# A two-network float32 forward pass on one core: norm chains by half blocks, a merged slab of narrow weights, and moved splits and dummy matmuls

## The reference

```
def rms_norm(x, gain):
    xf = x.astype(jnp.float32)
    y = xf * lax.rsqrt(jnp.mean(xf * xf, axis=-1, keepdims=True) + EPS)
    return (y * gain).astype(x.dtype)

# first network
for layer in range(2):
    hn = rms_norm(h, attn_norm[layer])
    h = h + (hgrn2_mixer(hn, ...) if layer == 0 else dsa_mixer(hn, ...))
    h = h + conv_ffn(rms_norm(h, ffn_norm[layer]), ...)      # SwiGLU with a conv of width 3
x = rms_norm(h, final_norm)

# second network
for l in range(2):
    g = norm_g[l]
    f = swiglu(rms_norm(h, g[0]), ffn1_w_in[l], ffn1_w_out[l])
    h = h + 0.5 * rms_norm(f, g[1])
    hn = rms_norm(h, g[2])
    m = even_mixer(hn, ...) if l == 0 else odd_mixer(hn, ...)
    h = h + rms_norm(m, g[3])
    f = swiglu(rms_norm(h, g[4]), ffn2_w_in[l], ffn2_w_out[l])
    h = h + 0.5 * rms_norm(f, g[5])
```

## Time and profile before

| | |
|---|---|
| median of 3 runs | 1748.61 us (1748.54 to 1750.45) |
| profiled execution | 1750.39 us, span 1748.6 us |
[...]
| instructions | 28885 |
| read from HBM | 280.88 MB, 161 GB/s over the span |

### The profile page before, as it was taken

How to read it: one execution, slowest core, us unless ns; L and a number is a source line. 1 busy time by engine, 2 the same in 40 slices (tenths; PEclk the granted TensorE clock), 3 DMA queues, 4 the chain that set the end, 5 groups by cost and what they waited for, 6 DMA issues and landing times. The chain is left out here.

```text
span 1748.6 us, 28885 instructions
## 1 busy us (share of the span) xinstructions
PE 1681.4 (96%) x11818; PEld 1565.9 (90%) x11818; DVE 1060.8 (61%) x1495; ACT 846.7 (48%) x1138; POOL 114.0 (7%) x37
## 2 busy tenths in 40 slices
PE   7999999999999999999999879999999999899998
PEld 6998999989799998999989669998999989889997
DVE  1796776756667676544569854555545575765544
ACT  6323655543555455544465364345543465363443
POOL 5351000020700000000010000000000000000000
PEclk9999999989999999999999989999999999999999
DMA  8622477733245555455553225555455654425552
GB/s 270 203 73 97 146 209 210 206 120 115 79 157 169 194 184 173 158 192 187 200 169 131 96 80 190 176 190 193 157 185 182 209 162 142 145 96 181 192 184 80
DMA packets 220068, 283.49 MB, mean 162 GB/s; under 512 B 13004, under 2 KB 197315, under 8 KB 219987
## 3 DMA queue, kind: packets, MB, share of 16 engines
q1 hardware_dynamic: 218499, 278.18, 48.9%
q10 hardware_dynamic: 1488, 4.17, 0.7%
HBM read 280.88 MB, written 1.44 MB: 161 GB/s over the span
## 5 line engine op out<-in xcount | busy, mean ns | idle before, releaser
L1616 PE MATMUL ps<-x_hi,w_hi 128*128 128x256 f32 (+1 forms) x2368 | 673.9, 285 | 1.0 <-DVE x_lo L1018 1.0
L1617 PE MATMUL ps<-x_lo,w_hi 128*128 128x256 f32 (+1 forms) x2368 | 672.4, 284 | 0.0
L1618 PE MATMUL ps<-x_hi,w_lo 128*128 128x256 f32 (+1 forms) x2368 | 672.2, 284 | 0.0
L546 ACT ACTIVATE w_hi<-raw 128x2048 fp32r<-128x2048 f32 x262 | 498.8, 1911 | 206.3 <-PE ps L1618 197.1
L1127 DVE TENSOR_TENSOR w_lo<-raw,w_hi 128x2048 fp32r<-128x2048 f32 x162 | 371.3, 2292 | 260.3 <-ACT w_hi L546 260.3
L1616 PEld LDWEIGHTS ps<-x_hi,w_hi 128*128 128x128 f32 (+1 forms) x2368 | 456.2, 193 | 5.4 <-issue 3.2
L1617 PEld LDWEIGHTS ps<-x_lo,w_hi 128*128 128x128 f32 (+1 forms) x2368 | 456.2, 193 | 2.3
L1618 PEld LDWEIGHTS ps<-x_hi,w_lo 128*128 128x128 f32 (+1 forms) x2368 | 456.0, 193 | 0.2
L1616 PE MATMUL ps<-w_hi,x_hi 128*128 128x256 f32 (+3 forms) x688 | 225.2, 327 | 27.1 <-DVE x_lo L1018 19.7
L1617 PE MATMUL ps<-w_lo,x_hi 128*128 128x256 f32 (+3 forms) x688 | 219.3, 319 | 0.0
L1618 PE MATMUL ps<-w_hi,x_lo 128*128 128x256 f32 (+3 forms) x688 | 219.3, 319 | 0.0
(11 more groups left out here) (170 smaller groups left out, 1334.8 us busy)
## 6 DMA issues: line engine op xcount, KB each, us to landing
raw<-in_ffn_w_in SPq DMA_DIRECT2D x88, 1024.0 KB, 5.1
raw<-in_ffn_w_up SPq DMA_DIRECT2D x44, 1024.0 KB, 5.1
raw<-in_ffn_w_out SPq DMA_DIRECT2D x44, 1024.0 KB, 4.8
raw<-in_ffn_w_down SPq DMA_DIRECT2D x22, 1024.0 KB, 5.0
raw<-in_hgrn_w_in SPq DMA_DIRECT2D x16, 1024.0 KB, 5.9
raw<-in_gla_w_in SPq DMA_DIRECT2D x12, 1024.0 KB, 5.5
raw<-in_hyb_w_in SPq DMA_DIRECT2D x10, 1024.0 KB, 5.6
raw<-in_dsa_w_in SPq DMA_DIRECT2D x6, 1024.0 KB, 5.6
```

What stands on the lines that cost most here:

```text
L546: act.activation(w_hi[slot][:, :], raw[slot][:, :], ACT.Copy).then_inc(hi_done[slot], 1)
L1616: pe.matmul(out_ap, a_hi, b_hi, start=start, stop=False, skip_group_check=True)
L1617: pe.matmul(out_ap, a_hi, b_lo, start=False, stop=False, skip_group_check=True)
L1618: return pe.matmul(out_ap, a_lo, b_hi, start=False, stop=stop, skip_group_check=True)
```

## The change

- **Norm chains.** Additions to h, gains, updates and squares go by halves of 512 columns, with new semaphores h_half, y_half and rms_eps. PE finishes the first half of a block's last product before the second and says so. The sum of squares is held in two columns; DVE adds eps to the first (`add_eps`), and ACT's root takes the second with that as its bias.
- **Order.** `split_normed(1)` on ACT comes ahead of the table preload and, in `normed_ffn`, `high_one(c_)` ahead of the second block's square. In `after_ffn` DVE gains or adds block 1 before it splits block 0. The last low part of an FFN is made in two halves, the second behind the norms (`low_part`).
- **Sparse attention.** Slot 0 holds w_idx (8 columns) beside v, slot 1 k_idx twice; one call projects 136 columns, DVE takes both out of one bank.
- **FFN 3's first two slabs** get their high and low parts at the end of the hybrid mixer; there the low part of slot 3 comes after all of the convolution, and ACT makes x_hi between the Silu steps.
- **GLA.** Low parts after steps 10, 11 and 13 become slots 2 and 3 after step 13 and slot 0 after the whole of `linear_attention`.
- **Dummies.** Those ahead of the transposes after FFN 1 to 4 are gone. New: 8 ahead of the outputs of each linear attention, 7, 2 and 9 after the first transposes of the three turned output projections, 6 at the end of the sparse attention, and in the hybrid mixer 18, 4, 8, 16 and 8 instead of 8, 4 and 8. In FFN 2 and 4 and in the mixers after them the second block's transposes move to before the last two of eight contraction steps.

The core of the diff:

```diff
-NEXT_PIECES = (3, 1, 1, 1, 1)
+NEXT_PIECES = (2, 1, 1, 1, 1)
...
-            load(0, [(raw_cols(0, 0, 64), ki), (raw_cols(0, 64, 64), ki), (raw_cols(0, P, P), col_slab(dsa_in, DSA_V, P))])
-            load(1, [(raw_cols(1, 0, IDX_HEADS), col_slab(dsa_in, DSA_W, IDX_HEADS))])
+            load(0, [(raw_cols(0, 0, IDX_HEADS), col_slab(dsa_in, DSA_W, IDX_HEADS)),
+                     (raw_cols(0, IDX_HEADS, P), col_slab(dsa_in, DSA_V, P))])
+            load(1, [(raw_cols(1, 0, 64), ki), (raw_cols(1, 64, 64), ki)])
...
+            def square_half(tb, part, src, scale):
+                at = 2 * tb + part
+                act.activation(squares[:, part * 512:part * 512 + 512], src, ACT.Square, scale=scale, accum_out=ssq[:, at:at + 1])\
+                    .then_inc(rms_sq, 1)
+            def root_of_sum(tb):
+                act.wait_ge(rms_sq, want(rms_sq, 2))
+                act.wait_ge(rms_eps, want(rms_eps))
+                act.activation(std[:, tb:tb + 1], ssq[:, 2 * tb + 1:2 * tb + 2], ACT.Sqrt, bias=ssq_eps[:, tb:tb + 1])\
+                    .then_inc(rms_std, 1)
...
                 split_normed(0, *norm)
                 if after_out and last is not None:
                     square_product(1, last, half)
+                high_one(c_)
                 square_h(1, updates)
+                split_normed(1, *norm)
                 preload(ACT.Silu)
-                high_one(c_)
-                split_normed(1, *norm)
...
+            split_normed(1, "norm_g_2", 0)
             preload(ACT.Silu)
             high_one(FFN_SLOTS[2][2])
-            split_normed(1, "norm_g_2", 0)
...
+                        if c >= 1:
+                            conv_high(c - 1)
+                    conv_high(3)
+                    high_one(FFN_SLOTS[3][0])
+                    high_one(FFN_SLOTS[3][1])
+                    preload(ACT.Sqrt)
...
+            def add_eps(tb, eps):
+                dve.wait_ge(rms_sq, want(rms_sq, 2) - 1)
+                dve.tensor_scalar(ssq_eps[:, tb:tb + 1], ssq[:, 2 * tb:2 * tb + 1], eps, None, ALU.add).then_inc(rms_eps, 1)
...
-                    gain_block(0, last)
+                    gain_block(0, last, 4.0 * EPS)
                     add_normed_block(0)
                     scaled_block(0)
-                    gain_block(1, last)
-                    split_normed(0, *norm)
-                    add_normed_block(1)
+                    gain_block(1, last, 4.0 * EPS)
                     if early is not None:
+                        low_part(d, 1)
+                        split_normed(0, *norm)
+                        add_normed_block(1)
                         low_one(early)
-                scaled_block(1)
-                split_normed(1, *norm)
+                    else:
+                        add_normed_block(1)
+                        split_normed(0, *norm)
+                        low_part(d, 1)
+                    scaled_block(1)
+                    split_normed(1, *norm)
...
-                                     {1: 2, 5: 3, 7: 0, 9: 1, 10: 2, 11: 3, 13: 0})
+                                     {1: (2,), 5: (3,), 7: (0,), 9: (1,), 13: (2, 3)})
+                    low_one(0)
...
             x0, x1 = x_new(), x_new()
             begin(0)
-            tokens(0, 0, P, P, SEQ, [0], x0)
+            tokens(0, 0, 0, IDX_HEADS + P, 0, [0], x0)
+            turn_block(1)
+            tokens(0, 0, 0, IDX_HEADS + P, 0, [1], x1).then_inc(slab_used[0], 1)
             begin(1)
-            tokens(1, 1, 0, IDX_HEADS, 0, [0])
-            turn_block(1)
-            tokens(0, 0, P, P, SEQ, [1], x1)
-            tokens(1, 1, 0, IDX_HEADS, 0, [1]).then_inc(slab_used[1], 1)
-            features(0, 0, 0, P, 0).then_inc(slab_used[0], 1)
+            features(1, 1, 0, P, 0).then_inc(slab_used[1], 1)
...
-                    keep_warm(2 * WARM_STEP)
+                    keep_warm(18)
...
+                pe.wait_ge(proj_free[3], made[3] + 1)
+                keep_warm(8)
                 pe.wait_ge(la_masked, want(la_masked, H // 2 + 2 * len(LEVELS)))
```

More of the change, by code:

```diff
@@ L594, in square_product @@
                     act.wait_ge(slab_used[last], ring.uses[last] + 1)
-                square(tb, ps[:, 2 * tb:2 * tb + 2, :].rearrange("p b n -> p (b n)"), half)
+                square_half(tb, 1, ps[:, 2 * tb + 1, :], scale)
+                root_of_sum(tb)
             def split_block(tb, groups, gains):
@@ L758, in fetch_gain, with normed_ffn @@
                 act.dma_start(gain_row, src.unsqueeze(0).broadcast_to([P, D])).then_inc(gain_in, 16)
-            def normed_ffn(f, norm, updates, conv=False, f_conv=0, after_out=True, last=None, half=False, gain=None):
+            def normed_ffn(f, norm, updates, conv=False, f_conv=0, after_out=True, last=None, half=False, gain=None, first=True):
                 a, b_, c_, _ = FFN_SLOTS[f]
@@ L958, in _ @@
                 out_last = (HYB_OUT, GLA_OUT)[l][RING - 1]
-                normed_ffn(3 + 2 * l, ("norm_g_2", l * 6 + 4), updates + 1, last=out_last, gain=A["norm_g_2"][l, 5])
+                normed_ffn(3 + 2 * l, ("norm_g_2", l * 6 + 4), updates + 1, last=out_last, gain=A["norm_g_2"][l, 5],
+                           first=l == 1)
                 if l == 0:
@@ L1037, in add_block, with gain_block, gain @@
             def add_block(tb, last):
-                product_done(tb, last)
-                dve.tensor_tensor(h[:, tb, :], h[:, tb, :], flat(2 * tb, 2), ALU.add).then_inc(h_ready, 1)
-            def gain_block(tb, last):
-                product_done(tb, last)
-                dve.wait_ge(rms_sq, want(rms_sq, 0) + 1)
-                for half in range(2):
+                for half, done in enumerate((h_half, h_ready)):
+                    at = slice(half * 512, half * 512 + 512)
+                    if half == 0:
+                        dve.wait_ge(y_half, want(y_half))
+                    else:
+                        product_done(tb, last)
+                    dve.tensor_tensor(h[:, tb, at], h[:, tb, at], flat(2 * tb + half), ALU.add).then_inc(done, 1)
+            def gain_block(tb, last, eps):
+                want(y_half)
+                def gain(half):
                     at = slice(half * 512, half * 512 + 512)
                     dve.tensor_tensor(xn[:, tb, at], flat(2 * tb + half), gain_row[:, at], ALU.mult).then_inc(y_gained, 1)
+                add_eps(tb, eps)
+                gain(0)
+                product_done(tb, last)
+                dve.wait_ge(rms_sq, want(rms_sq, 0))
+                gain(1)
             def add_normed_block(tb):
@@ L1067, in low_one, with low_part @@
                     .then_inc(slab_ready[slot], 1)
+            def low_part(slot, part):
+                at = slice(part * 1024, part * 1024 + 1024)
+                if part == 0:
+                    u, _ = lows.take(slot)
+                    dve.wait_ge(hi_done[slot], u + 1)
+                ins = dve.tensor_tensor(w_lo[slot][:, at], raw[slot][:, at], w_hi[slot][:, at].bitcast(F32), ALU.subtract)
+                if part == 1:
+                    ins.then_inc(slab_ready[slot], 1)
             def lows_elsewhere(n):
@@ L1071, in lows_elsewhere, with residual_ffn @@
                     lows.skip(s, n[s])
-            def residual_ffn(f, norm, out_slots, normed=False):
+            def residual_ffn(f, norm, out_slots, normed=False, first=True):
                 a, b_, _, _ = FFN_SLOTS[f]
@@ L1718, in project_out @@
                                         k == 0, k == NK - 1)
+                            if k == NK - 1 and half == 0:
+                                ins.then_inc(y_half, 1)
                         if tb == 0 and k == NK - 1:
@@ L1776, in up, with down_part @@
                     features(d, 5 + 2 * odd, P, P, SEQ).then_inc(slab_used[d], 1)
-                def down_block(s, tb, b, last, first=False):
-                    for half in range(2):
-                        hi, lo = (x_hi, x_lo) if last else (g_hi, g_lo)
-                        g = (hi[:, b, tb * P:tb * P + P], lo[:, b, tb * P:tb * P + P])
-                        ins = three(ps[:, 2 * tb + half, :], g, weights(s, b * D + half * 512, 512), first and b == 0,
-                                    last and b == 1)
-                    return ins
+                def down_part(s, tb, b, half, last, first=False):
+                    hi, lo = (x_hi, x_lo) if last else (g_hi, g_lo)
+                    g = (hi[:, b, tb * P:tb * P + P], lo[:, b, tb * P:tb * P + P])
+                    return three(ps[:, 2 * tb + half, :], g, weights(s, b * D + half * 512, 512), first and b == 0,
+                                 last and b == 1)
                 def down(i, first=False):
@@ L1790, in down @@
                         for b in range(2):
-                            ins = down_block(a, tb, b, False, first)
+                            for half in range(2):
+                                ins = down_part(a, tb, b, half, False, first)
                     ins.then_inc(slab_used[a], 1)
```

171 lines of the change are left out of this document (96 added, 75 removed).

## The result

| | before | after |
|---|---|---|
| median, us | 1748.57 (4 runs, 1747.46 to 1750.45) | 1721.51 (4 runs, 1719.56 to 1728.05) |
| profiled execution, its span | 1750.39, 1748.6 | 1720.02, 1718.2 |
| mean granted clock of PE (1.00 is full speed) | 0.982 | 0.992 |
| time at 0.50 in the profiled execution | 65.0 | 26.1 |

A forecast was written before the change was run, and what follows sets the result against it. PE, busy 96% of the span, was taken to bound the kernel. Place terms summed to -22.4 us, clock -6.0 and +4.2, together -24.2: from 1748.6 to 1724.4 us, range 1715 to 1737 at 8 in 10.

The forecast's parts named there:

- FFN 1 to 2: Between these FFNs: shorter norm chain, block 1's wait gone, new wait of about 2.2 for the token copy; net -2.5 us.
- mixer to FFN 3: Hybrid mixer into FFN 3: two slabs' high and low parts and the table load leave the chain; -6.1 us.
- FFN 3 to 4: Between these FFNs: eight dummies go, block 0's x_lo slightly later, block 1's 1.97 wait gone; -1.6 us.
- last block: End of kernel: square, gain and update by halves make 3.9 us to DVE's last step 3.0; -0.9 us.
- Part 1: Sparse attention: index weights beside the values remove 9.1 us of narrow matmuls and shorten the low clock; net -10.0 us.
- two ends: Sparse attention: slab queue 11.7 us earlier if the clock never drops, 9.5 if it drops once for some 10 us.
- counter-term: Sparse attention: chain starts 1.1 us sooner, but the split waits for PE's last product and PE idles some 1.1.
- held clock: Sparse attention, clock never dropping: GpSimd's low parts become the limit and PE waits 1 to 2 us for the first.
- Part 2: Norm chains by half blocks: steps overlap, 0.5 to 0.6 us go per pair; new eps step and new order on ACT.
- Part 3: GLA low parts moved: -1.8, new dummies +1.4, new wait of 1.8, shorter chain; +0.3 with the clock.
- Part 4: Dummies and clock: new dummies save four stretches of 3.4 us at 0.50, -6.0; dummies removed at transitions cost 4.2.
- bare gaps: Transitions without dummies: five places could get a stretch at 0.50; bounds 0 and 6.8 us, taken 4.2.

The follow-up runs named there:

- e10_old_order: The changed kernel with the earlier orders on ACT and DVE put back, halves, dummies and slab kept: 1718.35 us, ratio 0.9843.
- e4_gap_dummies: The changed kernel with eight dummies put back ahead of the first transposes of FFN 2, hybrid mixer, FFN 4 and GLA: 1720.12 us, ratio 0.9839.
- e8_gla_low: The changed kernel with DVE's low part of slot 0 in GLA made ahead of block 1's split: 1718.20 us, ratio 0.9838.

## Why the prediction was right, and where it wasn't

The forecast was 1724.4, of 24.2 us less; it is 1721.5, 27.1 less by the medians. The shape was right, and several terms that make it up are not what it said. Place by place, from PE's waits, dummies and starts in the two profiles (a place counts from the last product ahead of it; where it had a stretch at 0.50 within these bounds, that is in it):

| place | forecast | profiles |
|---|---|---|
| start and HGRN's dummies | +1.5 | +0.6 |
| FFN 0 and 1 entries | -0.8 | -0.9 |
| sparse attention | -10.0 | -11.2 |
| FFN 1 to 2 | -2.5 | -1.3 |
| FFN 2 to the mixer | +0.6 | -0.5 |
| mixer tail | -0.5 | -0.9 |
| mixer to FFN 3 | -6.1 | -5.4 |
| FFN 3 to 4 | -1.6 | -1.7 |
| FFN 4 to GLA | -0.1 | -0.2 |
| GLA | +0.3 | -0.3 |
| FFN 5 entry | -2.3 | -2.4 |
| last block | -0.9 | -0.9 |
| sum | -22.4 | -25.2 |

**Part 1, -10.0.** The stage lost 9.8, and 1.4 more with the wait of 1.30 ahead of its transposes at 370.64, which is gone. Alone the slab brings 8.4 to 8.6. Of the two ends, -11.7 if the clock never drops and -9.5 if it drops once for some 10 us, the prediction leaned on the second. Counted from FFN 0's last product, the changed kernel's first profile, with no drop, has -11.2; its second, with 10.2 us at 0.50, has -10.2. So both ends were seen, and they lie nearer together than forecast. The counter-term came as it was said: the chain starts sooner, and PE waits 1.13 for x_lo where it didn't. The GpSimd waits that were foreseen for the held clock came too (1.56 and 0.60). Over the eleven profiles of kernels with all or nearly all of the change it dropped in four (10.2 us three times, with whole blocks, with the old orders and in the changed kernel's second profile; 3.4 once). The step that was missed is small: the wait ahead of the values depends on part 2, so the two parts don't simply add.

**136 columns.** 24 matmuls of 136 columns take from 371.04 to 373.9, 0.12 us each; 8 and 128 columns stood at 0.11 and, at the low clock, 0.21. Taken as free, and they are, within 0.2 us.

**Part 2.** FFN 1 to 2: the new wait for the token copy was foreseen with 2.2 and is 1.83. But the printed parts of that term, 1.3 and 2.4 us of waits gone and 2.2 new, give -1.5 and not the -2.5 that went into the sum; the profiles have -1.3. PE's rows ahead of the first transposes, before and after, show the part that the dummies had in it:

```profile
691.85 1.90 PE L1694 MATMUL ps<-const 128*128 128x512 bf16 x8
694.99 1.09 PE L1702 MATMUL ps<-const,xn 128*128 128x128 f32 x8 [1.24 <-DVE xn L1029]
```

```profile
678.43 1.09 PE L1779 MATMUL ps<-const,xn 128*128 128x128 f32 x8 [1.69 <-DVE xn L1060]
```

Hybrid to FFN 3, -6.1: from the first transposes to the end of block 1's first weights it is 13.65 instead of 19.05 us, -5.4, of which 3.5 are waits and the rest clock. The size holds, the reason doesn't. The prediction said "Moved to where DVE waits ... they cost nothing"; undone, nothing is lost. The halves shortened this chain (with whole blocks 1.6 longer), and by the timelines the table load that moved out of it did too, which no run isolates; the low parts cost 1.3 in the mixer. The step that failed is the search for what is late next: the low parts had the wait in their name, and block 1's own chain ended just behind them, with a wait of 2.09.

The same holds for the orders. FFN 3 to 4 was forecast with -1.6 and is -1.7: the dummies' 1.74 go, and the two waits of 0.54 and 1.97 become one of 2.57. With the dummies gone the prediction has block 0's x_lo 0.35 later, a wait of 0.54 + 1.74 + 0.35 = 2.63, so the row agrees with it. But as causes the orders and the dummies fail: each undone, the time stays (e10_old_order, e4_gap_dummies), since the wait moves elsewhere in the same chain. The last block lost exactly what was said: from PE's last matmul to DVE's last step 3.0 instead of 3.9.

**Part 3.** The new wait in GLA was foreseen with 1.8 and is 1.72. The printed parts, -1.8, +1.4, +1.8, a chain 1.2 to 1.5 shorter and one stretch of 3.4 us less, give about -1.6 and not +0.3; the profiles have -0.3, nearer to the stated sum than to its parts. The eight dummies in HGRN cost 0.6 instead of 1.1.

**Part 4.** All four dummied places ran at 1.00, and in the profile without the dummies those at 475 and 1008 and the one in GLA didn't. The bare gaps were taken at 4.2, for four places without a stretch in the sum. In the kernel before the transitions had three already: at 707.8, at 1025.2 for 6.8 us, and at 1233.4, which the prediction doesn't mention, 13.6 us together. In the first profile of the changed kernel two of the five places had a stretch (6.8 us together, worth up to 3.4), in the second all five had one (17.0 us together, up to 8.5). Against before that is up to 3.4 less and up to 1.7 more. The mistake here was to treat the clock as a property of the kernel. The profile of before was itself one draw: 65.0 us at 0.50, and its 14 runs in one group lie between 1743.15 and 1750.34.

**The sum.** The places give -25.2 against -22.4; the sparse attention, FFN 2 to the mixer and the start are 3.2 better than forecast together, FFN 1 to 2 is 1.2 worse. They aren't work and waits alone: the sparse attention, FFN 3 and GLA have the clock of their places in them, on both sides. The profiles differ by 30.4, so -5.2 lie elsewhere, where the forecast had -1.8. There the stretches that went at the dummied places and in FFN 2, less the new one of 10.2 us in the mixer, are 6.8 us at 0.50 in all, worth up to 3.4. That the total was met within 3 us owes something to luck: single places miss by up to 1.2, two sums inside the terms don't come out, and the clock differs by up to 5 us between two profiles of the changed kernel (26.1 and 36.0 us at 0.50).

**The table switch.** ACT's timeline in FFN 2:

```profile
688.80 1.28 ACT L571 ACT_TABLE_LOAD   x1
690.10 0.20 ACT L571 ACTIVATE small<-small 128x1 f32<-128x1 f32 x1
690.21 1.89 ACT L546 ACTIVATE w_hi<-raw 128x2048 fp32r<-128x2048 f32 x1
692.01 0.58 ACT L633 ACTIVATE arena<-ps 128x512 f32<-128x512 f32 x1
```

The load took 1.28 us, the next instruction starts 0.02 us after it, and from the load's start to the high part's it is 1.41, where the prediction took 1.5. So in this place, and so in PE's wait of 1.83, the switch has the length of its load and nothing beyond it that the timeline shows.

What no run isolates: slab, halves and dummies account by their ratios for some 8, 6 to 9 and 1 to 4 us; the rest, some 6 to 12 us, is not assigned; it can lie in the table load, the GLA order and in how the parts act together on the clock.

## What to carry to other kernels

Thin work on the bound engine cost twice here, once as its own time and once as a low clock: taking 48 narrow matmuls away brought 8.4 us, and half of the low stretch went with them (10.2 us at 0.50 instead of 20.5). Dummies that keep the clock up are not free where the engine isn't waiting: here they saved up to 6 to 9 us of clock and took 4 to 5. When a wait has a culprit in its row, look at what would be late just behind it before crediting the edit: two of the moves here had the right size and no effect. And take several profiles before reading the clock: one kernel had 26 us at 0.50 in one execution and 36 in the next, in other places. The mean granted clock of every run, which needs no profile, tells clock from work better than one timeline does.

## What the runs showed of the hardware

**GpSimd and VectorE slow each other.** In after both make low parts at once. GpSimd's two (start, length):

```profile
378.46 4.60 POOL L469 TENSOR_TENSOR w_lo<-raw,w_hi 128x2048 fp32r<-128x2048 f32 x1 [240.12 <-ACT w_hi L546]
383.00 6.67 POOL L469 TENSOR_TENSOR w_lo<-raw,w_hi 128x2048 fp32r<-128x2048 f32 x1
```

DVE's start at 382.01 and 385.41 and take 3.19 and 6.40 where one alone takes 2.29. The ends fit turns: DVE's first ends at 385.20, 2.2 after GpSimd's first (383.0); GpSimd's second ends at 389.67, 4.5 after that, its length alone; DVE's second ends at 391.81, 2.1 after that. With 2.29 and 4.5 us for one alone, turns give these ends to within 0.2 us. That is a reading of this place; what the two share is not shown by any run. The prediction gave GpSimd's two 9.0 us; beside DVE they took 11.2, and DVE lost 5.0.

**How long the clock stays low.** The whole stretches at 0.50 seen in the fourteen profiles were 3.4, 6.8, 10.2 and 20.5 us long. Many came behind a wait of PE (707.8 in before, behind 2.40 us; 876.6 in after, behind 2.56); the longest lay over narrow matmuls with PE never idle. They didn't come every time: the same wait of 2.57 at the entry of FFN 4 has a stretch behind it in after and none in e8_gla_low.
